# Expert weights in six pieces per stretch of 896 features, and one loop over experts around one over stretches

## The reference, cut to what matters

```python
def swiglu_2(x, wg, wu, wd):
    return (jax.nn.silu(x @ wg) * (x @ wu)) @ wd

def moe_swiglu(x, router, wg, wu, wd):
    ...
    top_v, top_i = lax.top_k(logits, TOP_K)
    top_w = jax.nn.softmax(top_v, axis=-1)
    gate = jnp.sum(jax.nn.one_hot(top_i, N_EXPERTS, dtype=jnp.float32) * top_w[..., None], axis=1)
    y = jnp.zeros((bsz * s, d), jnp.float32)
    for e in range(N_EXPERTS):
        y = y + gate[:, e:e + 1] * swiglu_2(t, wg[e], wu[e], wd[e]).astype(jnp.float32)
    return y.astype(x.dtype).reshape(bsz, s, d)
```

## Time and profile before

| | |
|---|---|
| Time, median of 3 runs | 2854.03 us (2852.08 to 2854.36) |
| Span of the profiled execution | 2847.6 us; its own time is not shown apart, the median lies 6.4 us above the span |
| TensorE matmuls (PE) busy | 2739.6 us, 96% |
| TensorE weight loads (PEld) busy | 2198.6 us, 77% |
| VectorE (DVE), ScalarE (ACT) busy | 961.8 us (34%), 359.8 us (13%) |
| Moved by DMA | 620.42 MB, mean 218 GB/s |
| TensorE clock granted, mean | 0.986 |

### The profile page before, as it was taken

How to read it: one execution, slowest core, us unless ns; L and a number is a source line. 1 busy time by engine, 2 the same in 40 slices (tenths; PEclk the granted TensorE clock), 3 DMA queues, 4 the chain that set the end, 5 groups by cost and what they waited for, 6 DMA issues and landing times.

```text
span 2847.6 us, 80070 instructions
## 1 busy us (share of the span) xinstructions
PE 2739.6 (96%) x37718; PEld 2198.6 (77%) x37718; DVE 961.8 (34%) x1661; ACT 359.8 (13%) x775; POOL 18.5 (1%) x28
## 2 busy tenths in 40 slices
PE   8999998999999999999999999989999999999997
PEld 5777776687787666777657776569898998989997
DVE  2444444445645424554255443440000000000001
ACT  1210022100100112001240001510100000100000
POOL 1000000000000000000000000000000000000000
PEclk9999999999999999999999999899999999999999
DMA  7334412554534433444324444259999999999995
GB/s 197 133 133 150 160 60 103 202 178 153 181 134 149 164 118 124 145 163 149 116 104 158 169 164 134 101 194 380 381 394 365 396 374 369 397 369 375 385 378 211
DMA packets 307909, 620.42 MB, mean 218 GB/s; under 512 B 8886, under 2 KB 126908, under 8 KB 293212
## 3 DMA queue, kind: packets, MB, share of 16 engines
q1 hardware_dynamic: 304688, 606.13, 58.6%
q0 software_dynamic: 2400, 10.09, 1.2%
q10 hardware_dynamic: 588, 0.63, 0.1%
HBM read 615.77 MB, written 1.05 MB: 217 GB/s over the span
## 4 chain that ended last, share of the span: by engine, by line
PE 92%; DVE 3%; ACT 2%; issue 2%; DMA 1%; SPq 0%; DVEq 0%
PE ps L1807 19%; PE ps L1197 18%; PE ps L1124 13%; PE ps L1037 13%; PE ps L1823 9%; PE ps L1048 7%; PE ps L1720 2%; PE ps L1304 2%; PE ps L1782 1%; PE ps L1755 1%; ACT arena L891 1%; PE ps L1508 1%; DMA arena<-in_moe_w_up 1%; PE ps L1409 0%; PE ps L1518 0%
## 5 line engine op out<-in xcount | busy, mean ns | idle before, releaser
L1807 PE MATMUL ps<-arena,ring 128*64 128x88 f32 x10752 | 437.5, 239 | 18.0 <-issue 13.6
L1807 PEld LDWEIGHTS ps<-arena,ring 128*64 128x64 f32 x10752 | 422.0, 139 | 29.0 <-issue 22.9
L1124 PE MATMUL ps<-ring,arena 128*128 128x512 f32 x880 | 390.3, 597 | 0.0
L1037 PE MATMUL ps<-xT,ring 128*128 128x256 f32 (+2 forms) x1664 | 368.9, 382 | 2.9 <-DVE xT L1923 1.0
L1037 PEld LDWEIGHTS ps<-xT,ring 128*128 128x128 f32 (+2 forms) x1664 | 312.1, 188 | 59.4 <-issue 13.2
L2645 DVE TENSOR_TENSOR arena<-arena,ps 128x176 f32<-128x176 f32 x112 | 37.9, 338 | 826.6 <-ACT arena L907 826.6
L1124 PEld LDWEIGHTS ps<-ring,arena 128*128 128x128 f32 x880 | 163.2, 190 | 193.2 <-issue 193.1
L1823 PE MATMUL ps<-arena,ring 128*64 128x88 f32 x5376 | 226.9, 239 | 9.4 <-issue 9.3
L1823 PEld LDWEIGHTS ps<-arena,ring 128*64 128x64 f32 x5376 | 215.8, 137 | 12.4 <-issue 12.4
L1197 PEld LDWEIGHTS ps<-xT,ring 128*64 128x64 f32 x2816 | 155.8, 139 | 34.0 <-issue 33.7
L1197 PE MATMUL ps<-xT,ring 128*64 128x128 f32 x2816 | 166.6, 277 | 4.3 <-DVE arena L2040 3.5
(11 more groups left out here) (451 smaller groups left out, 2411.9 us busy)
## 6 DMA issues: line engine op xcount, KB each, us to landing
ring<-in_moe_w_gate SPq DMA_DIRECT2D x56, 2048.0 KB, 9.9
ring<-in_ffn_w_gate_up SPq DMA_DIRECT2D x88, 1024.0 KB, 7.7
ring<-in_moe_w_down SPq DMA_DIRECT2D x84, 1024.0 KB, 14.4
ring<-in_moe_w_up SPq DMA_DIRECT2D x28, 2048.0 KB, 14.5
arena<-in_moe_w_up SPq DMA_DIRECT2D x28, 2048.0 KB, 14.9
ring<-in_ffn_w_down SPq DMA_DIRECT2D x55, 1024.0 KB, 11.0
arena<-in_moe_w_down SPq DMA_DIRECT2D x28, 1024.0 KB, 10.1
ring<-in_fox_w_in SPq DMA_DIRECT2D x20, 768.0 KB, 6.1
```

Source lines behind the costliest of these rows:

```text
L1037: ins = pe.matmul(o, lhsT=w[:, k, c0:c0 + m], rhs=rhs[:, k, :], start=(k == 0), stop=(k == kt - 1))
L1124: return pe.matmul(ps[:, 4 + 2 * i + h, :], lhsT=h_par[:, s * S + i * P:s * S + (i + 1) * P], rhs=w[:, s, h * 512:(h + 1) * 512], start=(c ...
L1807: ins = pe.matmul(ps[h, par, c0:c0 + CAP], lhsT=w[:, k, s, h], rhs=xe[:, k, :], start=(k == 0), stop=(k == KD - 1))
```

## The change

**Pieces.** An expert is worked through in four stretches (`N_ST`) of `EW` = 896 features. Per stretch there are six pieces: gate rows 0 to 511, up rows 0 to 511, gate rows 512 to 1023, up rows 512 to 1023 (each 4 × 896 floats per partition, in pieces of 3,584 bytes), down for the first four tiles of 128 features (8 KB pieces) and for the last three (8 KB and 4 KB, two DMAs). Five lie in `ring`, the sixth in `arena`. Each has one loaded and one released semaphore and one place.

**Sweeps.** TensorE goes over each gate or up piece once (`sweep`, seven tiles × four × two halves = 56 matmuls): gate into banks 0 and 1, up into 2 and 3; the second half of the rows adds to the first. A piece is released by the first matmul of the sweep after it, the last one by its own last matmul. SiLU and the product are two instructions each per stretch, on four and on three tiles.

**Loops.** `Fori(0, N_EXP)` stands around `Fori(0, N_ST)`, so TensorE's code has one copy. `xe`, `gate_T` and `perm_w` have one buffer in place of two or eight, `perm` three places in place of eight: VectorE writes places for two experts ahead. At the end of expert `e` stand: scatter of `e - 1` (not for 0), gather for `e + 2` (not for the last two), turn of the places, turn of y. ScalarE copies the next expert's rows when `ex_released[3]` shows that the last sweep is over. Two gathers stand before the first expert.

```diff
+EW = 896
+ET = EW // P
+ET_A = 4
+ET_B = ET - ET_A
...
-        perm = cv(N_EXP, TT, CAP)
-        perm_w = cv(N_EXP, TT, CAP)
-        gate_T = cv(2, S)
-        xe_two = cv(2, KD, CAP)
+        perm = cv(N_EXP, TT, CAP)[:, 0:3]
+        perm_w = cv(N_EXP, TT, CAP)[:, 0]
+        gate_T = cv(2, S)[:, 0]
+        xe = cv(2, KD, CAP)[:, 0]
...
+        GU = 4 * EW
+        pieces = [ring_flat[:, j * GU:(j + 1) * GU] for j in range(4)]
+        pieces += [ring_flat[:, 4 * GU:4 * GU + ET_A * D], arena[:, LATE_AT:LATE_AT + ET_B * D]]
+        N_PIECES = len(pieces)
+        PIECE_SLOTS = [range(a // SLOT, (b - 1) // SLOT + 1) for a, b in
...
+            def expert_stretch(gate, up, down, f0, first):
+
+                def place(j):
+                    if first:
+                        place_free(j)
+                    else:
+                        sp.wait_ge(ex_released[j], t.up(f"ex_released{j}"))
+                for j, (w, kh) in enumerate(((gate, 0), (up, 0), (gate, 1), (up, 1))):
+                    place(j)
+                    sp.dma_start(pieces[j].rearrange("p (k n) -> p k n", n=EW),
+                                 w.rearrange("(k p) n -> p k n", p=P)[:, 4 * kh:4 * kh + 4, bass.ds(f0, EW)])\
+                      .then_inc(ex_loaded[j], 16)
+                place(4)
+                sp.dma_start(pieces[4].rearrange("p (q n) -> p q n", q=2),
+                             down[bass.ds(f0, ET_A * P), :].rearrange("(q p s) n -> p q (s n)", q=2, s=2))\
+                  .then_inc(ex_loaded[4], 16)
+                place(5)
+                sp.dma_start(pieces[5][:, 0:2 * D].rearrange("p (s n) -> p s n", n=D),
+                             down[bass.ds(f0 + ET_A * P, 2 * P), :].rearrange("(p s) n -> p s n", s=2)).then_inc(ex_loaded[5], 16)
+                sp.dma_start(pieces[5][:, 2 * D:3 * D], down[bass.ds(f0 + (ET - 1) * P, P), :]).then_inc(ex_loaded[5], 16)
...
+                    with act.Fori(0, N_ST) as i:
+                        t.enter(i, N_ST, {"gate_full": 2})
+                        for bank, c0, n in ((0, 0, ET_A), (1, ET_A, ET_B)):
+                            act.wait_ge(gate_full, t.up("gate_full"))
+                            act.activation(silu_e[:, c0 * CAP:(c0 + n) * CAP], ps[:, bank, 0:n * CAP], ACT.Silu)\
+                               .then_inc(silu_ready, 1)
                         t.leave()
-                    full()
+                    act.wait_ge(ex_released[3], t.up("ex_released3", N_ST))
                     if e < N_EXP - 1:
-                        xe_copy(e + 1)
-                    drain(gate_T_copy(e))
-                    full()
+                        drain(xe_copy())
...
+                def sweep(j, kh, b0, frees, full):
+
+                    pe.wait_ge(ex_loaded[j], t.up(f"ex_loaded{j}", EX_LOADS[j]))
+                    w = pieces[j].rearrange("p (k n) -> p k n", n=EW)
+                    w_pairs = w[:, :, 0:(ET - 1) * P].rearrange("p k (q n s) -> p k q s n", q=ET // 2, s=2)
+                    for f in range(ET):
+                        w_f = w_pairs[:, :, f // 2, f % 2] if f < ET - 1 else w[:, :, f * P:(f + 1) * P]
+                        bank, c0 = b0 + f // ET_A, f % ET_A * CAP
+                        for k in range(4):
+                            for h in HALVES:
+                                ins = pe.matmul(ps[h, bank, c0:c0 + CAP], lhsT=w_f[:, k, h], rhs=xe[:, 4 * kh + k, :],
+                                                start=(kh == k == c0 == 0), stop=(kh == 1 and k == 3), skip_group_check=True)
+                                if frees is not None and f == k == h.start == 0:
+                                    ins.then_inc(ex_released[frees], 1)
+                        if full and f in (ET_A - 1, ET - 1):
+                            ins.then_inc(full, 1)
...
+                def down(j, s0, n, frees):
+                    pe.wait_ge(ex_loaded[j], t.up(f"ex_loaded{j}", EX_LOADS[j]))
+                    pe.wait_ge(hid_ready, t.up("hid_ready"))
+                    w = pieces[j].rearrange("p (s n) -> p s n", n=D)
+                    for m in range(KD):
+                        o = ps[:, 4 + m // 4, (m % 4) * CAP:(m % 4 + 1) * CAP]
+                        for s in range(n):
+                            for h in HALVES:
+                                ins = pe.matmul(o[h], lhsT=w[:, s, m * P + h.start:m * P + h.stop],
+                                                rhs=hid_e[:, (s0 + s) * CAP:(s0 + s + 1) * CAP], start=False, stop=False,
+                                                skip_group_check=True)
+                                if m == s == h.start == 0:
+                                    ins.then_inc(ex_released[frees], 1)
+                    return ins
...
+                with pe.Fori(0, N_EXP) as e:
+                    adds = {f"ex_loaded{j}": N_ST * EX_LOADS[j] for j in range(N_PIECES)}
+                    adds.update(hid_ready=2 * N_ST, dve_to_pe=1)
+                    t.enter(e, N_EXP, adds)
+                    y_rows_read = e * 3 + d_act
+                    xe_next_read = e * 3 + (d_act + 1)
+                    yT_kept = e * 3 + (d_act + 2)
                     for b in (4, 5):
-                        ins = pe.matmul(ps[:, b, :], lhsT=zeros[0:1, 0:P], rhs=zeros[0:1, :], start=True, stop=False,
-                                        skip_group_check=True)
-                    if e > 0:
-                        y_tk = y_turn(yT_tk)
-                    if e == 0:
-                        pe.wait_ge(dve_to_pe, t.up("dve_to_pe"))
-                    if nth == e == 0:
-                        total = ps[:, 3, 0:N_EXP]
-                        for i in range(TT):
-                            ins = pe.matmul(total, lhsT=cst("ones"), rhs=route[:, 5, i], start=(i == 0), stop=(i == TT - 1))
-                        to_dve(ins, 3)
-                    gate_up()
-                    down()
-                    if e > 0:
-                        scatter(e - 1, y_tk, old_tk)
-                    with pe.Fori(0, M_ROUNDS) as i:
-                        adds = {f"ex_loaded{j}": 32 for j in range(0, M_RING, 2)}
-                        adds.update({f"ex_down_loaded{j}": 16 for j in range(M_RING)})
-                        adds.update(expert_chunk=M_RING, hid_ready=M_RING)
-                        t.enter(i, M_ROUNDS, adds)
-                        for _ in range(M_RING):
-                            gate_up()
-                            down()
+                        pe.matmul(ps[:, b, :], lhsT=zeros[0:1, 0:P], rhs=zeros[0:1, :], start=True, stop=False,
+                                  skip_group_check=True)
+                    with pe.Fori(0, N_ST) as i:
+                        adds = {f"ex_loaded{j}": EX_LOADS[j] for j in range(N_PIECES)}
+                        adds.update(hid_ready=2)
+                        t.enter(i, N_ST, adds)
+                        sweep(0, 0, 0, None, None)
+                        pe.wait_ge(drained_act, y_rows_read)
+                        sweep(1, 0, 2, 0, None)
+                        sweep(2, 1, 0, 1, gate_full)
+                        sweep(3, 1, 2, 2, up_full)
+                        down(4, 0, ET_A, 3)
+                        down(5, ET_A, ET_B, 4).then_inc(ex_released[5], 1)
                         t.leave()
-                    if e < N_EXP - 1:
-                        gather(e + 1)
-                    old_tk = xe_tk = to_act(turn_places(e), 6, 7)
-                    ins, last_slot_ = down(last=True)
-                    yT_tk = to_act(ins, 4, 5)
-                y_tk = y_turn(yT_tk, ex_down_released[last_slot_])
-                scatter(N_EXP - 1, y_tk, old_tk)
+                    with pe.If(e > 0):
+                        scatter()
+                    pe.wait_ge(dve_to_pe, t.up("dve_to_pe"))
+                    pe.wait_ge(drained_act, xe_next_read)
+                    with pe.If(e < N_EXP - 2):
+                        gather(0)
+                    turn_places()
+                    pe.wait_ge(drained_dve, e * 4 + d_dve)
+                    pe.wait_ge(drained_act, yT_kept)
+                    y_turn()
...
+                    if e > 1:
+                        add_rows()
                     if e > 0:
-                        add_rows()
-                    with dve.Fori(0, M_ROUNDS) as i:
-                        t.enter(i, M_ROUNDS, {"silu_ready": M_RING})
-                        for _ in range(M_RING):
-                            one()
+                        dve.wait_ge(places_used, t.up("places_used"))
+                        if e + 2 < N_EXP:
+                            find_places(0, e + 2)
+                        weigh_places(e)
+                    with dve.Fori(0, N_ST) as i:
+                        t.enter(i, N_ST, {"silu_ready": 2, "up_full": 2})
+                        for bank, c0, n in ((2, 0, ET_A), (3, ET_A, ET_B)):
+                            dve.wait_ge(silu_ready, t.up("silu_ready"))
```

(48 more changed lines are left out.)

182 lines of the change are left out of this document (53 added, 129 removed).

## The result

The changed kernel takes 2804.97 us (median of 4, 2802.16 to 2806.36), the kernel before on the same chip 2853.06 (4 runs). The ratio is 0.9831, 95% interval 0.9818 to 0.9845: 48 us or 1.7% less. Predicted were 2811 us in a range of 2804 to 2832.

A forecast was written before the change was run, and what follows sets the result against it. TensorE was taken to bound the expert pass, losing 45.8 us to code fetching, with DMA close behind; −40.8 − 3.7 + 1.0 − 0.8 + 1.6 = −42.7 from 2854.0 gives 2811 us. Own range 2804 to 2822; for 8 in 10, to 2832.

The forecast's parts named there:

- Pass over the code: TensorE, first expert: only the first pass through the new body stalls, six to seven packets at 0.62 us, say 5 us.
- Period: Expert pass of the changed kernel: time from one expert's start to the next, 110.2 us.
- The 0.2 for branches and register waits: TensorE's loops: branches and waits on registers taken at 0.2 us per expert, +1.6 us in all.
- 45.8 us go to code fetching: Kernel before, expert pass: TensorE's loss to fetching code, 6.1 + 36.0 + 3.7 us; 40.8 of it saved.
- the wait for rows: Expert boundary: TensorE waits 0.5 us for gathered rows; the copy becomes covered by down-products, 7 × 0.5 = 3.7 us saved.
- Loads: Weight loads in 3584 B packets at 400 GB/s: 108.4 us per expert against TensorE's 109.9, no wait on loads.
- S: Time in us that the loads of one stretch take; predicted 27.1 (27.7 to 26.2).
- The rival's formula: Slower loads: pass grows by 8 × (4 S − 109.9) − 13 us once positive; a little slower 0.10, as the bound 0.05.
- break-even at 377 GB/s: Loads as the bound of the expert pass: from S = 29.2 they eat the gain of 43 us; chance 0.05.
- The body fetched again: TensorE's new body fetched again per expert: 6.5 packets × 0.62 × 7 = +28 us, 2839 us; chance 0.06.
- The two-page rule: Jumps back outside a two-page window: each inner round fetches five pages anew, +96 us, 2907 us; chance 0.02.
- the holes were waits for weights: TensorE's holes on issue: fetches go but the holes stay, time about 2850 us; chance 0.04.

The follow-up runs named there:

- the written-out kernel: Changed kernel with TensorE's outer loop undone, the eight experts written out, each with its own inner loop over four stretches: 2827.48 us, ratio 0.9911 to the kernel before.
- half the bytes: Changed kernel with two of the four 128-row blocks of each later gate/up piece left unloaded: 2802.38 us; the same edit with experts written out: 2803.33 us.
- a body of 7.5 packets: Changed kernel with the gather at the outer loop's end written four times in place of once, 480 matmuls in the outer body: 2922.23 us.
- all three longer bodies: Changed kernel with two stretches in the inner body: 3063.08 us; with the outer loop's end gather written four times: 2922.23 us; six times: 2945.72 us.

## Why the prediction was right

*Direction, mechanism and time* held: 2804.97 lies in the range, near its lower end. The central claim, that the body stays on the engine and the packets cost only in its first pass, is shown by the rows above and by the written-out kernel. How far a body may grow was not known, and there the forecast had some luck (below).

*Pass over the code.* Predicted 6 to 7 packets and 5 us in the first expert; there are 7, three holes of 2.9 us together, and 4.0 us of its period (110.2 against 106.3 of work; 106.4 with half the bytes).

*Period.* Predicted 110.2, measured 110.04. The 0.2 for branches and register waits was not needed.

*The term that was mis-sized* is "45.8 us go to code fetching". Fetching cost about 39; I had put down to it all that exceeded the work and the wait for rows. The rest, with the 3.7 for that wait about 10 us in all, I put down to the old order with its restarts, of which the new has fewer. Both went, so the sum of −42.7 came out close to the measured −44.7 of the pass however the two are divided: fetching 39 − 4 = 35, and 10 for the order. (That these two add up to the measured time is no proof of them, as the 10 were got by subtraction.) What lies beyond, 3.4 us, is the part ahead of the pass (2.6 between the two profiled executions) and the spread of the medians.

*Loads.* S was predicted at 27.1 and is 26.8; "no wait on loads" is true. The rival's formula overstated the slack: it has 4 us for S = 28.0, and 17.3 were measured. Its break-even at 377 GB/s is therefore too low as well, though no run came to it; with 393 the gain shrinks from 48 to about 32 us.

*The body fetched again,* to which I gave 6%, was nearer than that. "The old loop has the same size" was a sound reason, and the only one: a body of 7.5 packets is fetched again in every expert. The price of that rival was too low too: 4.0 us in each of seven experts, where the body of 7.5 packets pays about 9.

*The two-page rule* of the Trainium skill ("Runtime: NRT & Kernel Launch", instruction fetch mechanics) doesn't hold for this engine's loops of up to 6 packets. Beyond the limit the traces agree with the stall that it describes, 6.12 us at one jump back. The same section gives TensorE's instruction memory as 128 KiB; no run shows a body of more than 96 KiB (1,536 instructions) staying, and one of 120 KiB (1,920) doesn't.

The rival that *the holes were waits for weights* fell with the changed kernel and the written-out one. Both have the same loads and the same order of work under full traffic, and the holes come and go with the packets of code. (The run with half the bytes doesn't tell the two apart, as it relieves both.) The rival was half right in one thing: weight traffic is what makes the code late.

## What to carry to other kernels

With weights streaming at full rate, every 16 KB of new instructions on TensorE cost 0.4 to 0.7 us here in written-out code, and up to 1.2 where a loop jumped back to code that it had to fetch again; part of that was the lower clock behind a long hole. Look for holes on "issue" spaced by a constant count of instructions and for the instruction queue's row in the DMA view. Make one loop body of all that repeats and keep it near 1,500 instructions: one of 1,920 was fetched again in every round, and all three longer bodies here, their added work taken off, were slower than the written-out kernel. Count the swing inside a period, not only the mean rate, when you ask how much slack a ring of loads has.

## What was not expected of the hardware

- Loads of 1,792-byte and of 896-byte packets both ran at 393 GB/s in this mix, those of 3,584 bytes at 411.
- The 50 code packets of the written-out kernel were free under two thirds of the weight traffic (no hole), and cost 20 us under all of it. The 80 of the kernel before still left 7.6 us of holes at two thirds; why was not tried.
- After a hole of some 6 us TensorE was granted 0.50 of its clock for another six to eight us, so that a long stall cost more than its own length.
- A body of 7.5 packets of 16 KB makes TensorE fetch 9 packets per round of the outer loop, more than the body holds; why more was not tried.
- The residency limit lies between 6.0 and 7.5 packets. Where exactly, and whether it depends on where the body starts within a packet, stays open.
